# Prologue of a two-block transformer kernel: modulation sums moved to one-column products on TensorE, early weight splits to GpSimd

## The reference

```python
c_act = jax.nn.silu(c)                         # (1, 1024)
mod = c_act @ w_ada[l] + b_ada[l]              # (1, 1024) @ (1024, 6144)
sh1, sc1, g1, sh2, sc2, g2 = jnp.split(mod, 6, axis=-1)
h = modulate(rms_norm(x, norm1_w[l]), sh1, sc1)   # norm * (1 + sc1) + sh1
p = h @ w_in                                   # q, k, v, z, a, beta, ...
```

## Time and profile before

| | |
|---|---|
| median of three timed runs | 2207.74 us |
| the profiled execution's own time | 2205.96 us |
| its span in the profile | 2204.2 us |
| mean granted clock of TensorE, as a share of 2.4 GHz | 0.989 |
| TensorE busy | 2145.2 us, 97% of the span |
| VectorE busy | 1319.4 us, 60% |
| ScalarE busy | 859.6 us, 39% |
| GpSimd busy | 428.6 us, 19% |

### The profile page before, as it was taken

The page is one execution under the profiler, slowest core; times in us unless marked ns, Lnnn a source line. Parts: engine busy times, 40 slices in busy tenths (PEclk is TensorE's granted clock), DMA queues, the critical chain, the costliest instruction groups (busy, mean ns, idle before and its releaser), DMA issues.

```text
span 2204.2 us, 30270 instructions
## 1 busy us (share of the span) xinstructions
PE 2145.2 (97%) x10504; PEld 1773.6 (80%) x10504; DVE 1319.4 (60%) x1886; ACT 859.6 (39%) x1352; POOL 428.6 (19%) x331
## 2 busy tenths in 40 slices
PE   6999999999999989999999999999899999999998
PEld 4788888888888878888888888888677777888886
DVE  6777777777644453344557655643688867555431
ACT  3333333332232232332235454522566635545321
POOL 0356765557700300000110000011000000000021
PEclk8999999999999999999999999999999999999999
DMA  8434333344333323333332333233112122333332
GB/s 288 113 106 123 106 98 110 106 114 114 96 89 114 115 81 99 95 95 91 95 116 61 99 99 99 82 99 104 51 58 58 53 82 86 95 95 95 91 96 72
DMA packets 394816, 216.96 MB, mean 98 GB/s; under 512 B 7880, under 2 KB 391298, under 8 KB 393219
## 3 DMA queue, kind: packets, MB, share of 16 engines
q1 hardware_dynamic: 393939, 213.64, 33.1%
q0 software_dynamic: 288, 2.10, 0.3%
q10 hardware_dynamic: 528, 0.40, 0.1%
HBM read 211.92 MB, written 4.19 MB: 98 GB/s over the span
## 4 chain that ended last, share of the span: by engine, by line
PE 87%; DVE 7%; ACT 2%; issue 1%; DMA 1%; SPq 1%; POOL 0%; POOLq 0%; ACTq 0%; DVEq 0%
PE ps L2114 25%; PE ps L2116 25%; PE ps L2115 25%; PE ps L2287 5%; PE ps L2141 3%; DMA ada<-w_ada 1%; DVE w_lo L1251 1%; DVE small L1998 1%; DVE a_t_lo L2007 1%; DVE a_sb L2031 1%; ACT at_swap L1154 1%; ACT prob L1177 0%; PE ps L2583 0%; DVE prob L2026 0%; PE ps L2584 0%
## 5 line engine op out<-in xcount | busy, mean ns | idle before, releaser
L2114 PE MATMUL ps<-h_hi,w_hi 128*128 128x512 f32 x1896 | 769.9, 406 | 10.5 <-DVE h_lo L1315 5.5
L2116 PE MATMUL ps<-h_hi,w_lo 128*128 128x512 f32 x1896 | 743.0, 392 | 0.0
L2115 PE MATMUL ps<-h_lo,w_hi 128*128 128x512 f32 x1896 | 741.5, 391 | 0.0
L1251 DVE TENSOR_TENSOR w_lo<-raw,w_hi 128x1024 fp32r<-128x1024 f32 x336 | 435.2, 1296 | 362.2 <-ACT w_hi L772 362.0
L772 ACT ACTIVATE w_hi<-raw 128x1024 fp32r<-128x1024 f32 x336 | 355.5, 1059 | 633.4 <-PE ps L2116 583.4
L2114 PEld LDWEIGHTS ps<-h_hi,w_hi 128*128 128x128 f32 x1896 | 358.9, 189 | 82.0 <-issue 13.8
L2116 PEld LDWEIGHTS ps<-h_hi,w_lo 128*128 128x128 f32 x1896 | 357.7, 189 | 77.3
L2115 PEld LDWEIGHTS ps<-h_lo,w_hi 128*128 128x128 f32 x1896 | 359.4, 190 | 65.0
L2114 PE MATMUL ps<-act_hi,w_hi 128*128 128x512 f32 x528 | 208.5, 395 | 0.0
L2116 PE MATMUL ps<-act_hi,w_lo 128*128 128x512 f32 x528 | 207.0, 392 | 0.0
L2115 PE MATMUL ps<-act_lo,w_hi 128*128 128x512 f32 x528 | 205.0, 388 | 0.0
(11 more groups left out here) (361 smaller groups left out, 2705.2 us busy)
## 6 DMA issues: line engine op xcount, KB each, us to landing
raw<-ffn_w_up SPq DMA_DIRECT2D x88, 512.0 KB, 3.8
raw<-w_in SPq DMA_DIRECT2D x72, 512.0 KB, 3.8
raw<-w_ffn_in SPq DMA_DIRECT2D x44, 512.0 KB, 3.8
ada_w<-w_ada SPq DMA_DIRECT2D x32, 512.0 KB, 4.1
raw<-ffn_w_down SPq DMA_DIRECT2D x32, 512.0 KB, 3.7
raw<-diff_w_qkv SPq DMA_DIRECT2D x24, 512.0 KB, 3.8
ada<-w_ada SPq DMA_DIRECT2D x8, 1024.0 KB, 13.2
ada_w<-w_ada_f SPq DMA_DIRECT2D x16, 512.0 KB, 4.0
```

What stands on the lines that cost most here:

```text
L1251: nc.vector.tensor_tensor(w_lo[:, tile.slot], raw[:, tile.raw], w_hi[:, tile.slot].bitcast(F32), SUB)\
L2114: nc.tensor.matmul(dst, w_hi[:, tile.slot, k], hi, start=first, stop=False)
L2115: nc.tensor.matmul(dst, w_hi[:, tile.slot, k], lo, start=False, stop=False)
L2116: return nc.tensor.matmul(dst, w_lo[:, tile.slot, k], hi, start=False, stop=last)
```

## The change

1. The first ten of the sixteen 128-column tiles of the modulation are made on TensorE as one-column products: for every k and each of the ten, the 128x128 block of ada0[k] is the stationary operand and c_act's column k moves, and the result is added up over k in one column of bank 1. VectorE multiplies and adds the other six (768 columns instead of 1536), which TensorE turns as before. The row in bank 4, ScalarE's copy of it and the four products with a single row are gone.
2. The splits of tiles 4 to 8 move from VectorE to GpSimd, one after another, ahead of head 0. Each waits for hi_ready of its tile and for lo_ready of the one before. VectorE waits for lo_ready of tile 8 before head 0.
3. z is in bank 5 instead of bank 0, and TensorE waits in every head for out_used[5] to be at least 1 before it writes banks 5 and 6.

```diff
@@ -238,7 +238,7 @@
     x_kept = nc.dram_tensor("x_kept", (P, KD, T), F32, kind="Internal").ap()
     stream = Stream()
     AB = stream.stage(1, [0])
-    QKVZ = stream.stage(4, [1, 7, 6, 0])
+    QKVZ = stream.stage(4, [1, 7, 6, 5])
     HEAD = stream.stage(8, [0, 1, 0, 7, 1, 0, 6, 1], H - 1)
     LAST = stream.stage(12, [0, 1] * 6)
     GATE = stream.stage(8, [0, 1] * 4, 2)
@@ -276,6 +276,7 @@
         return KD * SCALED_NORMS.index(r)
 
     AB_LINKS = 26
+    ADA_PE = 10
 
     O_BANK = (3, 5, 3, 5)
 
@@ -684,6 +685,12 @@
 
             factor(N_MIX)
 
+            for tile in [AB.tile(0, 0).ahead()] + [QKVZ.tile(t, 0).ahead() for t in range(4)]:
+                pool.wait_ge(hi_ready, tile.before + 1)
+                pool.wait_ge(lo_ready, tile.before)
+                nc.gpsimd.tensor_tensor(w_lo[:, tile.slot], raw[:, tile.raw], w_hi[:, tile.slot].bitcast(F32), SUB)\
+                  .then_inc(lo_ready, 1)
+
             def head(h):
                 own = [24 * h + 1]
 
@@ -864,9 +871,6 @@
                 squares = nc.scalar.activation(o_tok[:, n], x_tok[:, n], ACT.Square,
                                                accum_out=small[:, S_SQX + n:S_SQX + n + 1])
             squares.then_inc(x_sq, 1)
-
-            act.wait_ge(pro_row, 1)
-            nc.scalar.activation(ada0_sum[0:1, 0:T], bank(4)[0:1], ACT.Copy).then_inc(ada_row, 1)
 
             split(Tile(2))
             act.wait_ge(mod_ready, 1)
@@ -1355,9 +1359,9 @@
             split(Tile(1))
             for m in range(2, KD, 2):
                 x_copy(m)
-            total = ada0_sum[:, T:4 * T]
+            total = ada0_sum[:, ADA_PE * P:2 * D]
             for k in range(KD):
-                src = ada0[:, k, T:4 * T]
+                src = ada0[:, k, ADA_PE * P:2 * D]
                 dve.wait_ge(ada_in[k], 16)
                 if k == 0:
                     nc.vector.tensor_scalar(total, src, cact[:, 1, k:k + 1], None, MULT).then_inc(ada0_own, 1)
@@ -1426,7 +1430,6 @@
 
             dve.wait_ge(ab_pe, 1)
             link(nc.vector.tensor_copy(v, bank(2)[:, 0:2 * H * NC].rearrange("p (n c) -> p n c", n=NC)))
-            split(AB.tile(0, 0).ahead())
             conv_silu(0, 0)
 
             dve.wait_ge(ab_act, 2)
@@ -1448,7 +1451,6 @@
             link(nc.vector.tensor_tensor(s6.rearrange("p n (two h) -> p n two h", two=2), s5.rearrange("p n (two h) -> p n two h", two=2),
                                         alog[:].unsqueeze(1).unsqueeze(1).to_broadcast([P, NC, 2, H]), MULT))
             conv_taps(QKVZ, 1, 0, 1, 0)
-            split(QKVZ.tile(0, 0).ahead())
             conv_silu(1, 0)
 
             link(nc.vector.tensor_scalar(s2, e, 1.0, None, ADD))
@@ -1468,10 +1470,8 @@
             dve.wait_ge(g_dve, 1)
             dve.sem_inc(g_dve, ahead_of_heads(DVE_STEPS) - 1)
             conv_silu(2, 0)
-            split(QKVZ.tile(1, 0).ahead())
-            split(QKVZ.tile(2, 0).ahead())
             z_silu(QKVZ, 3, 0, 0)
-            split(QKVZ.tile(3, 0).ahead())
+            dve.wait_ge(lo_ready, QKVZ.tile(3, 0).ahead().before + 1)
 
             def head(stage, i, h):
                 more = stage is HEAD
@@ -2229,18 +2229,16 @@
             pe.wait_ge(pro_dve, 5)
             for k in range(KD):
                 pe.wait_ge(ada_in[k], 16)
-                row = nc.tensor.matmul(bank(4)[0:1], cact[:, 1, k:k + 1], ada0[:, k, 0:T], start=k == 0, stop=k == KD - 1)
-                if k == KD - 1:
-                    row.then_inc(pro_row, 1)
+                for j in range(ADA_PE):
+                    nc.tensor.matmul(bank(1)[:, j:j + 1], ada0[:, k, P * j:P * j + P], cact[:, 1, k:k + 1],
+                                     start=k == 0 and j == 0, stop=k == KD - 1, skip_group_check=True)
                 if k == 5:
                     pe.sem_inc(n_pe, 1)
                     rows(N_MIX)
             pe.wait_ge(ada0_own, KD)
-            for j in range(4, 16):
-                nc.tensor.matmul(bank(1)[:, j:j + 1], ada0_sum[:, P * j:P * j + P], one_col, start=True, stop=True)
-            pe.wait_ge(ada_row, 1)
-            for j in range(4):
-                s = nc.tensor.matmul(bank(1)[:, j:j + 1], ada0_sum[0:1, P * j:P * j + P], ones[0:1, 0:1], start=True, stop=True)
+            for j in range(ADA_PE, 16):
+                s = nc.tensor.matmul(bank(1)[:, j:j + 1], ada0_sum[:, P * j:P * j + P], one_col, start=False, stop=True,
+                                     skip_group_check=True)
             s.then_inc(pro_pe, 1)
 
             pe.wait_ge(mod_ready, 1)
@@ -2300,6 +2298,7 @@
                 fill("kk_qk")
 
                 pe.wait_ge(g_dve, last_head("o_gate", h))
+                pe.wait_ge(out_used[5], 1)
                 by_chunk(5, k_s, k_s)
                 by_chunk(6, k_s, q_s).then_inc(g_pe, 1)
                 fill("kb_rows")
```

## The result

The changed kernel takes 2220.59 us (median of four runs, 2219.87 to 2221.3) against 2207.44 us: a ratio of 1.006 with a 95% interval of 1.0048 to 1.0072, so 13.2 us slower. The forecast was 2218.3. The profiled execution has a span of 2218.9 us, 14.7 more than before.

What follows compares the result with a forecast made beforehand. TensorE, busy for 97% of the span, was taken to bound the kernel. The profiled 2205.96 us + 15.6 (prologue) - 5.1 (head 0's start), with 1.8 for the median, gave 2218.3 us; range 2211 to 2224.

Steps and rivals of the forecast that it cites:

- the signs named for a right forecast: Clock 0.50 from before 27 to beyond 55 us, modulation read near 56; no idle or cold stretch before head 0; lo_ready early.
- The price of a pass and the fall of the clock: Prologue stream from 19.1 us: one-column passes cost 0.11 us while the clock holds for 2.3 us, then 0.22.
- The first term: Prologue: the one-column products fall behind at the low clock and delay the modulation; +15.6 us, bounds +9.5 to +17.8.
- The smaller share of VectorE and the start of h: Prologue: VectorE ending 0.9 us sooner earns nothing with TensorE behind; h again starts cold, up to 2.3 us either way; 0.
- The second term: Start of head 0: z in bank 5 and splits on GpSimd remove TensorE's idle and cold stretches; -5.1 us, bounds 0 to -7.4.
- two of VectorE's splits ahead of it ... 2.4 us, so about 73.2: Before head 0: without two splits in VectorE's chain, the v activation ends near 73.2 us instead of 75.7.
- The idle 3.43 us: TensorE's wait at the start of head 0 for z to leave bank 0; claimed to go entirely, 3.43 us.
- tile 8's earlier split: Ahead of head 0: GpSimd finishes splitting tile 8 at 78.4 us where VectorE had it at 83.2, gaining 4.8 us.
- the 35.7 forecast: Ahead of head 0: ScalarE's half of tile 8, behind z, was forecast at 75.9 us in the old kernel's times.
- The sum: Whole kernel: +15.6 us for the prologue and -5.1 us for head 0's start, giving 2218.3 us with the median's 1.8.
- GpSimd late: Rival at head 0: slow stream as forecast, but the wait for tile 8 takes VectorE's gain away; 2223.4 us, chance 0.13.
- The rival by the rule of idle gaps: Rival in the prologue: an unbroken one-column stream keeps 2.4 GHz, so the change is faster; 2201.0 us, chance 0.16.

Runs made afterwards that it cites:

- products: The changed kernel with VectorE's five splits and z in bank 0 put back, leaving only the one-column modulation products; 2218.7 us, ratio 1.0055.
- splits: The kernel before with only the five splits moved to GpSimd and z in bank 5, modulation sums unchanged; 2207.63 us, ratio 1.0003.
- side_two: The kernel before plus five unread two-input GpSimd additions on scratch at the moments of the changed kernel's splits; 2208.92 us, ratio 1.001.
- side_one: The kernel before plus five unread one-input GpSimd multiplications by a constant at the moments of the changed kernel's splits; 2208.16 us, ratio 1.0004.
- bank: The kernel before with only z moved to bank 5, the splits staying with VectorE; 2207.79 us, ratio 1.0002.
- warm: The kernel before plus 20 unread wide passes on TensorE in its idle time in the prologue; 2204.44 us, ratio 0.9984.
- order_keep: The kernel before with z in bank 5, VectorE and ScalarE reordered, four modulation tiles as one-column products, unread wide passes between; 2200.45 us, ratio 0.9968.
- wide: The changed kernel plus two unread 512-column products among the one-column products of every row block, 32 passes more; 2247.19 us, ratio 1.0179.
- bank with the order: The kernel before with z in bank 5 and VectorE's and ScalarE's operations reordered, all splits on VectorE; 2202.82 us, ratio 0.9981.

## Why the prediction was right, and where it wasn't

The sign, the size and the cause of the loss were right, but that the total came within 3 us is partly luck: one of the two terms had the wrong sign, and other differences made up for more than half of it. Of the signs named for a right forecast, the first came (clock 0.50 from before 27 us, modulation read at 53.96); the other two, no idle time and no low stretch ahead of head 0 and a wait for lo_ready that ends in time, did not (4.13 us, 3.4 us at 0.51, and 2.46 us). Point by point:

- **The price of a pass and the fall of the clock.** Forecast 0.11 and 0.22 us, clock held for 2.3 us, stream from 19.1 us; measured 0.108 and 0.21 us, 2.9 us (18.9 to 21.8), 18.9 us. The reading that did it was that the clock fell in the middle of a stream of such passes. That 2.3 us came so near 2.9 is luck: it was 4.3 us in products.
- **The first term, +15.6 us: measured +13.77.** The mechanism is right. The size is 1.8 us too large, in small parts: the stream began 0.2 us sooner, the clock held 0.6 us longer (worth 0.7 us), the remaining 145 slow passes took 31.3 us instead of 31.9, and the four transposes 0.9 us instead of 1.1.
- **The smaller share of VectorE and the start of h, 0:** VectorE ended long before TensorE; h stayed at the low clock for 5.8 instead of 4.6 us, which costs 0.6 us, since an h product takes 0.43 us from start to start there and 0.23 at the upper level.
- **The second term, -5.1 us, failed: measured +1.93** from the trace of before to that of the changed kernel, +0.5 from that of products (0.6 of the +1.93 is the longer start of h at the low clock), and no gain in splits. The step that failed is "two of VectorE's splits ahead of it ... 2.4 us, so about 73.2". The splits did leave VectorE's chain, but it got back 2.13 + 1.82 us of standing at two small operations, and 0.7 us twice of waiting for ScalarE's tanh (the splits had covered that wait). I had treated GpSimd and VectorE as independent engines. The trace of before shows that they aren't, in GpSimd's and VectorE's rows of head 0, which I had not used:

```profile
92.41 2.88 POOL L692 TENSOR_TENSOR ada_w<-ada_w,cact 128x1024 f32<-128x1024 f32 x1
```

```profile
94.61 0.70 DVE L1580 TENSOR_TENSOR small<-small 128x4 f32<-128x4 f32 x1
```

VectorE's operation on 128x4 elements takes 0.70 us and ends at 95.31, with GpSimd's at 95.29; another of that size (L1528) takes 0.16. It is so in all eight heads: L1580 takes 0.70 to 1.08 us. The Trainium skill's page "SBUF — State Buffer", in the section "Who interferes with whom", calls the port pair that GpSimd shares with VectorE an exclusive lock, held for a whole instruction; side_two agrees (1.06 and 0.76 us), and side_one doesn't fully, as VectorE ran inside GpSimd's one-input operation (0.23 us from 62.66). The runs show the waiting; that its place is a port, none of them shows.
- **z in bank 5.** The idle 3.43 us moved, as bank shows, to the next two places where TensorE needs VectorE in head 0 (L1538, 3.1 us, and the u product L1555, 0.5 us). The forecast had counted on tile 8's earlier split to clear that, and it came through GpSimd only at 98.7 us, 44.8 us behind the modulation; VectorE had it at 43.0 before. Two causes add up: ScalarE's half of tile 8 ended at 95.49, 41.5 us behind the modulation and not at the 35.7 forecast, as it stands behind the v tanh, which waits for VectorE; and GpSimd, still at tile 7, needed 3.2 us more, where VectorE had needed 1.3.
- **The sum.** +15.6 - 5.1 = +10.5 against +13.2. Two errors of opposite sign: the first term 1.8 us too large, the second 7.0 us too good; against them stand the -1.0 us behind head 0 and a difference of the medians that is 1.5 us smaller than that of the profiled spans (14.7). The -1.0 and the 1.5 are explained by no run, so part of the agreement in the total is luck. The rival "GpSimd late" (2223.4 us, chance 0.13) had the better place for the second term, though it put it down to GpSimd's longer operation alone.
- **The rival by the rule of idle gaps** (2201.0 us) is out: the stream had no gap and ran at 0.50 for 32 us. warm and order_keep show that the clock can stay up through such passes, with other work among them or ahead of them; wide shows that such work doesn't always do it.

## What to carry to other kernels

Price a TensorE pass at the clock that the new stream itself will get, and read that from what the engine did just before each fall of the granted clock; one-column products with fresh weights cost 0.11 or 0.21 us a pass here, and the second is what the long streams of them got. Before moving work to an idle GpSimd, look in the trace for short VectorE operations that end together with a GpSimd operation; they price the move. Where a wait goes, do the next engine's order by hand as well: bank alone gave nothing, bank with the order gave 3.8 us (the order alone, with z in bank 0, was not run).

## What the runs showed of the hardware that I had not expected

- Unread products in idle time made the kernel faster: 20 wide passes, -3.5 us (warm). They can also cost: 32 wide passes among the changed kernel's one-column products, where the clock fell all the same, cost 26.6 us (wide).
- Two-input work on GpSimd held a 0.2 us VectorE operation for up to 2.35 us, to GpSimd's own end; one-input work held small operations for 0, 0.2 and 0.6 us (side_one).
- The clock in the prologue falls at another moment in each execution, even where the kernels are the same up to there: at 21.8 us in the changed kernel's profile and at 23.0 in products, at 27.3 in the kernel before and at 33.6 in side_two.
